# The second block's output product as three fp32r products, with split branches in the merge

## The reference

```python
def first_block(x, c, ...):
    mod = silu(c) @ ada_w + ada_b            # 6 x 1024: shift1, scale1, gate1, shift2, scale2, gate2
    h = rms_norm(x, norm_mix_w) * (1 + scale1) + shift1
    proj = h @ w_in                          # 8-head attention and a gated linear recurrence
    ya, yh = o_att @ w_branch_att, o_hg @ w_branch_hg       # 512 -> 1024 each
    merged = sigmoid(g0) * ya + sigmoid(g1) * yh
    x = x + gate1 * (merged @ w_out)
    h = rms_norm(x, norm_ffn_w) * (1 + scale2) + shift2
    return x + gate2 * expert_choice_ffn(h, ...)   # 16 experts, 64 tokens each, 1024 -> 2048 -> 1024

def second_block(x, ...):
    z = rmsnorm(x, g_mix) @ w_in + b_in
    y = concat(conv_group(z), pool_group(z))       # 512 + 512 features
    h = x + y @ w_out                              # 1024 x 1024, the product of this change
    h = h + swiglu(rmsnorm(h, g_ffn), ...)         # 1024 -> 2816 -> 1024
    return rmsnorm(h, g_final)
```

## Time and profile before

| | us |
|---|---|
| median of 3 runs | 2107.97 (2107.93 to 2111.01) |
| profiled execution | 2108.66 |
| its span, first to last instruction | 2106.9 |
| TensorE busy | 1923.8 (91%) |
| VectorE busy | 670.3 (32%) |
| ScalarE busy | 448.6 (21%) |
| HBM read | 510.00 MB, 243 GB/s over the span |

### The profile page before, as it was taken

How to read it: one execution, slowest core, us unless ns; L and a number is a source line. 1 busy time by engine, 2 the same in 40 slices (tenths; PEclk the granted TensorE clock), 3 DMA queues, 4 the chain that set the end, 5 groups by cost and what they waited for, 6 DMA issues and landing times.

```text
span 2106.9 us, 20424 instructions
## 1 busy us (share of the span) xinstructions
PE 1923.8 (91%) x8738; PEld 1153.0 (55%) x8738; DVE 670.3 (32%) x931; ACT 448.6 (21%) x673; POOL 28.7 (1%) x41
## 2 busy tenths in 40 slices
PE   5999989999689999898988998888899999999998
PEld 5876766567444343343434334342344588888887
DVE  5474474475411110202011010201129623222333
ACT  5357446212211000010100001010020313222222
POOL 0000000000000000000000000000030000000000
PEclk9999999999889999999999999999999999999999
DMA  7311210584669999999999999999951032332311
GB/s 296 97 44 41 63 38 21 202 283 174 259 253 416 417 418 418 417 416 417 416 416 417 418 418 417 417 416 416 380 163 60 20 100 85 96 100 100 100 60 40
DMA packets 149183, 513.42 MB, mean 244 GB/s; under 512 B 8035, under 2 KB 74723, under 8 KB 114147
## 3 DMA queue, kind: packets, MB, share of 16 engines
q1 hardware_dynamic: 144720, 487.95, 59.3%
q10 hardware_dynamic: 4374, 24.18, 3.0%
HBM read 510.00 MB, written 2.10 MB: 243 GB/s over the span
## 4 chain that ended last, share of the span: by engine, by line
PE 67%; DMA 21%; DVE 6%; ACT 4%; issue 2%; SPq 0%; POOL 0%; ACTq 0%; DVEq 0%; POOLq 0%
DMA work<-in_w_exp_up 13%; PE ps L1100 11%; PE ps L1061 6%; DMA ring<-in_w_exp_up 6%; PE ps L1263 5%; PE ps L521 5%; PE ps L1222 4%; PE ps L1223 4%; PE ps L1224 4%; PE ps L537 3%; PE ps L539 3%; PE ps L538 3%; PE ps L988 3%; PE ps L544 3%; PE ps L720 2%
## 5 line engine op out<-in xcount | busy, mean ns | idle before, releaser
L1061 PE MATMUL ps<-work 128*64 128x512 f32 x1208 | 331.4, 595 | 34.9 <-DMA work<-in_w_exp_up 34.9
L1061 PE MATMUL ps<-ring,work 128*64 128x512 f32 x720 | 218.8, 595 | 19.8 <-DMA ring<-in_w_exp_up 19.8
L1061 PEld LDWEIGHTS ps<-work 128*64 128x64 f32 x1208 | 112.0, 137 | 209.5 <-issue 142.3
L2167 DVE TENSOR_TENSOR work<-work,ps 64x512 f32<-64x512 f32 x64 | 42.0, 692 | 495.2 <-ACT work L1629 494.5
L1629 ACT ACTIVATE work<-ps 64x512 f32<-64x512 f32 x64 | 32.6, 584 | 751.1 <-PE ps L1061 751.1
L521 PE MATMUL ps<-work,ring 128*128 128x512 f32 x320 | 138.9, 592 | 0.7 <-issue 0.7
L1100 PE MATMUL ps<-work 128*64 128x512 f32 x568 | 135.4, 630 | 4.2 <-issue 3.6
L1061 PEld LDWEIGHTS ps<-ring,work 128*64 128x64 f32 x720 | 71.7, 137 | 122.8 <-issue 84.4
L1222 PE MATMUL ps<-xh,wh 128*128 128x512 f32 x352 | 137.0, 389 | 0.0
L1224 PE MATMUL ps<-xh,wl 128*128 128x512 f32 x352 | 136.9, 389 | 0.0
L1223 PE MATMUL ps<-xl,wh 128*128 128x512 f32 x352 | 136.9, 389 | 0.0
(11 more groups left out here) (311 smaller groups left out, 2531.7 us busy)
## 6 DMA issues: line engine op xcount, KB each, us to landing
work<-in_w_exp_gate SPq DMA_DIRECT2D x76, 1024.0 KB, 24.5
work<-in_w_exp_up SPq DMA_DIRECT2D x75, 1024.0 KB, 25.9
work<-in_w_exp_down SPq DMA_DIRECT2D x71, 1024.0 KB, 21.0
ring<-in_w_exp_gate SPq DMA_DIRECT2D x45, 1024.0 KB, 24.5
ring<-in_w_exp_up SPq DMA_DIRECT2D x45, 1024.0 KB, 25.5
ring<-in_w_exp_down SPq DMA_DIRECT2D x42, 1024.0 KB, 22.0
ring<-in_w_in SPq DMA_DIRECT2D x27, 1024.0 KB, 6.4
work<-in_ada_w ACTq DMA_DIRECT2D x16, 1024.0 KB, 6.1
```

Of the source, the lines that this page charges most:

```text
L1061: i = e.matmul(PS[64 * gu:64 * gu + 64, fb, :], at(XET + 128 * k + 64 * z, 64), flat(key)[:, 512 * fb:512 * fb + 512], start=(k == 0), sto ...
```

## The change

The second output product takes the split form. Its weights come as four pieces of 512 rows by 512 columns, are cut by ScalarE and VectorE into `O2H` and `O2L`, and y is written twice by ScalarE, raw and high, with the low half from VectorE over the raw tile. The product runs by halves of columns and then tiles of tokens, in the order of tiles `Y_ORDER`; the last pool product moves into its first unit. The branch products of the merge take the same form: `cb_hi`, `cb_lo` split the weights, `OHH`/`OHL` and `OAH`/`OAL` hold the halves of the inputs. The ada row and column products of d = 6 move behind the first two units of the first output product. Half of x is loaded later. The slots' order changes for the experts and the tail. The last expert's down weights go by halves of columns, in rows of 2 KB.

Slots, order of the tail, and SyncE:

```diff
-    cycle = (12, 13, 14, 15, 8, 16, 2, 4, 7, 11, 9, 10, 1, 5, 3, 0, 6)
+    cycle = (2, 13, 12, 16, 15, 8, 7, 11, 14, 4, 9, 10, 1, 5, 3, 0, 6)
...
-    tail = [("i2", c) for c in (3, 1, 2, 0, 5, 4)] + [("o2", n) for n in range(4)] + [("ff", f) for f in range(33)]
-    slots += [0, 1, 2, 3, 4, 5, 0, 1, 2, 3] + [(4, 0, 1, 2, 3)[f % 5] for f in range(33)]
+    tail = [("i2", 3), ("i2", 1), ("o2", 0), ("o2", 1)] + [("i2", c) for c in (2, 0, 5, 4)] + [("o2", 2), ("o2", 3)] + [("ff", f) for f in range(33)]
+    slots += [0, 1, 13, 15, 2, 3, 4, 5, 0, 1] + [4, 5, 4, 5] + [f % 5 for f in range(29)]
...
                 if key == ("wo", 0):
-                    e.wait_ge(s["mg_m"], 1)
+                    e.wait_ge(s["mg_pb"], 6)
...
-                    r0, c0 = 512 * (key[2] % 4), 256 * (key[2] // 4)
-                    for dh in range(2):
-                        src = t["w_exp_down"][NE - 1, r0:r0 + 512, 512 * dh + c0:512 * dh + c0 + 256].rearrange("(k p) n -> p k n", p=128)
-                        e.dma_start(piece(key)[:, 4 * dh:4 * dh + 4, :], src).then_inc(ring[slot], 16)
+                    r0, c0 = 512 * (key[2] % 4), 512 * (key[2] // 4)
+                    src = t["w_exp_down"][NE - 1, r0:r0 + 512, c0:c0 + 512].rearrange("(k p) n -> p k n", p=128)
+                    e.dma_start(piece(key, 4), src).then_inc(ring[slot], 16)
```

TensorE:

```diff
+            def branch(bk, half, j, off, hi, lo, each=None):
+                wl = FWL[plan["cb", half][0]]
+                for k in range(4):
+                    if each is not None:
+                        each(k)
+                    w, x = slice(256 * (off + k) + 128 * j, 256 * (off + k) + 128 * j + 128), slice(512 * k, 512 * k + 512)
+                    e.matmul(bank(bk), CBH[half][:, w], hi[:, x], start=(k == 0), stop=False)
+                    e.matmul(bank(bk), CBH[half][:, w], lo[:, x], start=False, stop=False)
+                    p = e.matmul(bank(bk), wl[:, w], hi[:, x], start=False, stop=(k == 3))
+                return p
...
                     dense_w(b0 + 1, k1, j).then_inc(s["mg_gb"], 1)
-                kb = ("cb", half)
...
                 if j == 0:
-                    e.wait_ge(*got[kb])
-                if d == 6:
...
+                    e.wait_ge(s["fs_l"], (2, 4, 5, 6)[half])
...
+                    e.wait_ge(s["sx_l"], 2)
+                    branch(b0 + 3, half, j, 4, OHH, OHL).then_inc(s["mg_pb"], 1)
+                    branch(b0 + 2, half, j, 0, OAH, OAL, lambda k: e.wait_ge(s["sx_l"], 3 + k)).then_inc(s["mg_pa"], 1)
+                    continue
...
+                branch(b0 + 2, half, j, 0, OAH, OAL).then_inc(s["mg_pa"], 1)
+                if d >= 2:
                     e.wait_ge(s["mg_b"], d - 1)
...
+                branch(b0 + 3, half, j, 4, OHH, OHL).then_inc(s["mg_pb"], 1)
...
+            def second_gate(u):
+                if u == 0:
+                    e.wait_ge(s["d_ada"], 16)
+                    e.wait_ge(s["mg_a"], 8)
+                    ada_row(ACC1, 0, 6)
+                    e.wait_ge(s["mg_b"], 8)
+                    ada_row(ACC1, 512, 7)
+                elif u == 1:
                     e.wait_ge(s["ar_a"], 1)
                     ada_cols(ACC1, 1, 6, 0).then_inc(s["ac_pe"], 1)
...
-            for h in range(2):
-                for n in range(4):
...
+            for a in range(2):
+                for tc in range(TC):
+                    u = 4 * a + tc
+                    o2_free(u)
+                    for n, k in enumerate(Y_ORDER):
+                        q = 2 * a + k // 4
+                        if tc == 0 and n in (0, 2):
+                            e.wait_ge(s["fs_l"], FS_O2 + 2 * a + 2)
+                        if u == 0:
+                            if n == 4:
+                                pool_out(15, 0)
+                            e.wait_ge(s["sx_l"], SXL_O2 + n + 1)
+                        o, w, bk = 128 * tc, slice(512 * (k % 4), 512 * (k % 4) + 512), (0, 1, 2, 3, 6, 7)[u % 6]
+                        e.matmul(bank(bk), YH[:, 512 * k + o:512 * k + o + 128], O2H[q][:, w], start=(n == 0), stop=False)
+                        e.matmul(bank(bk), YH[:, 512 * k + o:512 * k + o + 128], O2L[q][:, w], start=False, stop=False)
+                        p = e.matmul(bank(bk), y_low(k)[:, o:o + 128], O2H[q][:, w], start=False, stop=(n == KD - 1))
                     p.then_inc(s["o2_pe"], 1)
```

ScalarE:

```diff
+            def cb_hi(half, o, n):
+                e.wait_ge(*got["cb", half])
...
+                    e.wait_ge(s["lv_pe"], 52)
+                    e.wait_ge(s["lv_og"], 4)
+                else:
+                    e.wait_ge(s["mg_m"], 4 if half == 2 else 2)
+                e.activation(CBH[half][:, o:o + n], flat(("cb", half))[:, o:o + n], ACT.Copy).then_inc(s["fs_h"], 1)
...
+            def branch_hi():
+                for o in (0, 1024):
+                    cb_hi(0, o, 1024)
+                    yield
+                for o in (0, 1024):
+                    e.activation(OHH[:, o:o + 1024], at(OHG + o, 1024), ACT.Copy).then_inc(s["sx_h"], 1)
+                    yield
...
-            e.dma_start(at(X, 4096).rearrange("p (c d) -> p c d", c=4), xv).then_inc(s["l_x"], 16)
+            e.dma_start(at(X + 2048, 2048).rearrange("p (c d) -> p c d", c=2), xv[:, 2:4, :]).then_inc(s["l_x"], 16)
+            for o in (0, 1024):
+                cb_hi(1, o, 1024)
...
             for d in range(4, 8):
                 i = d - 4
-                if d == 7:
-                    wo_hi(0)
...
                 elif d >= 6:
                     e.wait_ge(s["mg_m"], d - 1)
                 e.activation(at(mt[4 * (d % 2)], 512), bank(4 * (d % 2)), ACT.Tanh, scale=0.5).then_inc(s["mg_sa"], 1)
+                if d in (4, 6):
+                    cb_hi(d // 2, 0, 2048)
+                elif d == 7:
+                    wo_hi(0)
...
+            def o2_hi(i):
+                e.wait_ge(*got["o2", i])
+                if i < 2:
+                    e.wait_ge(s["x_ym"], 34)
+                else:
+                    e.wait_ge(s["i2_pe"], 8)
+                e.activation(O2H[i], flat(("o2", i)), ACT.Copy).then_inc(s["fs_h"], 1)
+            o2_hi(0)
+            o2_hi(1)
...
+                e.activation(YH[:, 2048 + 512 * g:2560 + 512 * g], bank(u % 4), ACT.Copy, scale=vcol("spool", g)).then_inc(s["sx_h"], 1)
                 e.activation(at(YP + 512 * g, 512), bank(u % 4), ACT.Copy, scale=vcol("spool", g)).then_inc(s["po_y"], 1)
...
             for i in range(4):
                 e.wait_ge(s["y_d"], i + 1)
+                e.activation(YH[:, 512 * i:512 * i + 512], at(CV + 512 * i, 512), ACT.Silu, bias=vcol("lnb", i), scale=vcol("lng", i)).then_inc(s["sx_h"], 1)
                 e.activation(at(YC + 512 * i, 512), at(CV + 512 * i, 512), ACT.Silu, bias=vcol("lnb", i),
                              scale=vcol("lng", i)).then_inc(s["y_a"], 1)
-            pool_in(13, 0, 12)
+                if i == 1:
+                    pool_in(13, 0, 12)
             pool_out(14, 1)
             pool_out(15, 0)
```

VectorE:

```diff
+            def cb_lo(half, o, n, count):
+                e.wait_ge(s["fs_h"], count)
+                e.tensor_tensor(FWL[plan["cb", half][0]][:, o:o + n], flat(("cb", half))[:, o:o + n], CBH[half][:, o:o + n].bitcast(F32),
+                                ALU.subtract).then_inc(s["fs_l"], 1)
...
+            for pair in range(4):
+                x = slice(512 * pair, 512 * pair + 512)
+                e.wait_ge(s["at_o"], pair + 1)
+                e.tensor_tensor(OAL[:, x], at(OATT + 512 * pair, 512), OAH[:, x].bitcast(F32), ALU.subtract).then_inc(s["sx_l"], 1)
+            for i in range(2):
+                cb_lo(1, 1024 * i, 1024, i + 3)
...
                     two_ada(d)
+                    if d in (4, 6):
+                        cb_lo(d // 2, 0, 2048, d // 2 + 3)
...
+            def y_lo(*ns):
+                for n in ns:
+                    k = Y_ORDER[n]
+                    e.wait_ge(*((s["y_a"], k + 1) if k < 4 else (s["po_y"], 8 - k)))
+                    e.wait_ge(s["sx_h"], SXH_O2 + n + 1)
+                    e.tensor_tensor(y_low(k), y_raw(k), YH[:, 512 * k:512 * k + 512].bitcast(F32), ALU.subtract).then_inc(s["sx_l"], 1)
+            o2_lo(0)
+            o2_lo(1)
...
+            y_lo(0, 1)
...
+            y_lo(2, 3)
             pool_window(0)
+            y_lo(4, 5, 6, 7)
```

More of the change, by code:

```diff
@@ L119, in ring_plan @@
         n += key[0] != "ada"
-    i = more.index(("c0", 3))
+    i = len(more)
     keys += more[:i] + [("wo", 0)] + more[i:] + [("wo", i) for i in range(1, 4)]
-    slots.insert(len(slots) - len(more) + i, 16)
+    slots.insert(len(slots) - len(more) + i, 14)
     slots += [4, 5, 0]
@@ L1600, in _ @@
             wo_hi(1)
-            for k in range(2, 8):
+            for k in range(2, 7):
                 merged_hi(k)
+            e.wait_ge(s["mg_pa"], 8)
+            e.dma_start(at(X, 2048).rearrange("p (c d) -> p c d", c=2), xv[:, 0:2, :]).then_inc(s["l_x"], 16)
+            merged_hi(7)
             wo_hi(2)
```

(25 more changed lines are left out.)

169 lines of the change are left out of this document (81 added, 88 removed).

## The result

| | before | after |
|---|---|---|
| median, us (7 runs each) | 2108.66 | 2115.28 |
| span of the profiled execution, us | 2106.9 | 2113.8 |
| mean granted TensorE clock | 0.970 | 0.964 |

The ratio is 1.0028, with a 95% interval of 1.0018 to 1.0038: 0.3% slower, 6.6 us. The forecast was 2110.5 us, with a range of 2101.5 to 2118 and 0.33 for slower by over 0.2%; its likeliest case was no measurable change. So the sign of its sum was right, its size 4 us short.

The account below looks back on a forecast made before the run. Bounds by stage: mostly TensorE, the ada loads and VectorE steps early in the merge, weights in the experts. +13.8 - 5.7 + 5 + 1.5 + 3.5 = +18.1, then -15.5: taken as +2.5, 2110.5 us, range 2101.5 to 2118.

Parts of the forecast that it names:

- Merge, d=4: Branch product of d=4 starts at 449.8 us, behind ada step 17 and its weight's split: +13.8 us, attention tail counted in.
- d=0 to 3 gain nothing: Merge: the shorter branch products of d=0 to 3 only lengthen TensorE's wait for the low half at 428.7: 0.
- Merge, d=6: Wait before the d=6 branch products for the split behind ada step 21, its load beside `wo` 0: +5 us.
- Output product: First output product: moved ada row and column products cost 0; first unit waits for the fifth tile's low half, +1.5 us.
- Experts one for one: Experts stay at 60.2 us each, paced by weights; a later start ends the kernel later by the same time.
- Second output product: Second block's output product: 43.5 us in place of 55.51, earlier start, shorter work behind it; -15.5 us in all.
- Last down weights: Last expert's down product is TensorE's own work and waits for no weights: value 0, bounds 0 and -0.4 us.
- Clock: Slow matmuls behind the two new TensorE waits cost 2.1 and 1.4 us: +3.5 us.
- The splits arrive in time: Rival: the merge's low halves are ready as TensorE comes, so nothing is lost: 2088 us, chance 0.06.
- The ada chain shortens: Rival: step 17 comes at 442 and the d=6 wait shrinks to 2 us: 2102.5 us, chance 0.14.
- The product gains less: Rival: ScalarE's doubled writes and VectorE's low halves hold the second output product's first unit 4 us more: 2114.5 us, chance 0.08.
- The waits cost more: Rival: d=6 wait of 7.5 to 8 us, clock low about 7 us after both waits: 2116.3 us, chance 0.22.

Follow-up runs that it names:

- e4: The changed kernel with branch weight 2's split moved: high half before the load of ada 16, low half between ada steps 14 and 15; 2098.1 us, ratio 0.9939.
- e7: e4 with the 32 one-column ada products parted, 16 behind the second unit of the first output product and 16 behind the third; 2100.3 us, ratio 0.9953.
- e2: The kernel before with only the new merge and what goes with it, without the new second output product and last down weights; 2129.5 us, ratio 1.0090.
- e1: The kernel before with only the second output product changed; 2094.7 us, ratio 0.9924.
- e12: e9 with the d=6 second gate piece's low halves ahead of the d=5 merge, and both halves of y at multiples of 64 bytes; 2087.3 us, ratio 0.9896.
- e3: The kernel before with only the last expert's down weights going by halves of columns in rows of 2 KB; 2111.1 us, ratio 1.0004.
- e8: e4 with the two low halves for the gate products of d=4 made between ada steps 12 and 13 on VectorE; 2100.0 us, ratio 0.9960.
- e10: e1 with the two low halves for the gates of d=4 made between ada steps 12 and 13 on VectorE; 2094.6 us, ratio 0.9924.
- e5: e4 with the low half of branch weight 3 ahead of ada steps 20 and 21 on VectorE; 2095.7 us, ratio 0.9937.
- e6: e5 with the loads of ada 20 and 21 issued behind the high half of branch weight 3 on ScalarE; 2094.9 us, ratio 0.9932.
- e9: The changed kernel with the edits of e5 to e7 and the other merge splits moved ahead of ada steps; 2091.3 us, ratio 0.9910.

## Why the prediction was right or wrong

**Merge, d=4: right.** 449.8 us forecast, 450.22 measured, after ada step 17 at 445.49 (445.1 forecast) and a low half of 2.29 us. e4 shows that the queue was the cause. The first ada load of the chain starts at 395.15 instead of 393.74, 1.4 us later where +1.0 stood for the attention's tail, and takes 11.40 us instead of 13.95; which part of the change made it shorter was not tested.

**d=0 to 3 gain nothing: right**, by the wait that grew from 2.47 to 7.18 us.

**Merge, d=6: size within its bounds, cause half wrong.** The wait is 3.62 us, within the +3 to +7.5 given around +5. The step said that ada 21 would hold the low half, because `wo` 0 would make its load take 10 to 12 us. The chain of the changed kernel says otherwise:

```profile
474.95 9.72 DMA ring<-in_w_branch_hg
484.69 1.92 ACT cbh L1559
486.70 2.31 DVE fwl L2087
489.05 0.79 PE ps L877
```

Step 21 started 8.3 us after its load was issued (474.31) and was over at 484.95. What came last was the branch weight's own load, 9.72 us beside 3 MB of ada and output weights, and then both halves in series. An estimate from these rows: behind step 21 alone the low half would have ended at 487.2, and TensorE came at 485.43, so 1.8 of the 3.62 us are the step's and the rest is the load's. That step 21 starts 32.4 us after the d=4 product, within the forecast 31.2 to 33.2, is luck: its load went out 24.1 us after that product, not 21.2, and was faster than forecast.

**Output product: the term that failed.** The ada row and column products "only move behind the output product's first units: 0". They do move, and the sum up to the first unit is right: 13.8 - 5.7 + 5 + 3.5 less the 3.4 us of products that leave d=6 is 13.2, and the unit starts at 512.57 instead of about 499.6, 13 us later. (The closeness is in part luck: the wait of d=6 was 1.4 us shorter than its term and the d=4 start 0.5 us later than its own.) The wait in the first unit is 1.39 us, near the +1.5. But at their new place both groups of 16 one-column products stand together, and 2.2 us of slow matmuls follow; before, each group of 16 stood alone (480.06 and 511.06 us) and nothing slow followed. e7 shows the difference in the rows. The groups together take 4.1 us where two took 1.7 us each, 0.7 us more. With 0.8 us in the routing (the last unit's addition is 20.8 us late, the gather 21.6) that makes 3.7 us, against the 3.5 us between +18.1 and +21.6 before the experts. The products of this step were put at 0 without a row for their new place; they cost 2.9 us.

**Experts one for one: right.** 21.6 us at the first gather, 21.4 at the last down product, 60.2 us per expert. e2 shows that nothing of it comes back.

**Second output product: mechanism right, one term mis-sized.** -15.5 forecast, -14.1 measured in the whole change, -14.0 in e1. A unit takes 5.60 us, not 5.44: 8 by 0.16 = 1.3 us. The wait in the first unit is 0.2 us instead of 0.6. From the last product to the transposes it takes 3.24 us (1738.65 to 1741.89), where 3.25 was forecast. On the product alone the rows forecast 12.0 us; eight units of 5.60 us save 10.7, and eight of 5.44 us (e12) would save the 12.0. The estimate by the four passes of the Trainium skill, page "FP8 and Floating Point Precision", section "TensorE Precision Notes", was 13.9 us of 55.51; no run reached it. What the overhead is that the prediction gives as the reason is not shown: the rows give 0.227 us for an fp32r matmul and 0.859 us for a plain one, no more.

**Last down weights: right**, 0 (e3), though they land at 395 instead of 341 GB/s.

**Clock.** After the two waits of 12.27 and 3.62 us there are 9 and 6 steps of 0.43 us, at a granted clock of 0.50, 1.8 and 1.2 us lost, near the 2.1 and 1.4 of the sum. What it lacked was the third place, behind the one-column products.

**The rivals.** "The splits arrive in time" gave 2088 us, and it is what the reordered kernels reach (2091.3 and 2087.3): its mechanism was right for another order of the same instructions, which the prediction didn't weigh. "The ada chain shortens" did not come: step 17 is at 445.49, not 442. "The product gains less" did not either, for its reason: the first unit waits 0.2 us, and what is missing is the 1.3 us of the addresses. "The waits cost more" named the d=6 split as the place and 2116.3 us; the time is near it, the place is not.

## What to carry to other kernels

A product in a cheaper form needs its operands split first, and the split runs on in-order engines: before counting the gain, find what stands ahead of each split in VectorE's and ScalarE's lists, and put it ahead of those that wait for a load. Where TensorE waits at several places for one in-order chain, moving one split alone may only move the wait (e8, e10); e4 paid because the wait that it removed, 12.27 us, was far longer than what came back behind it (0.88 us). The edits after e4 are worth 1 to 4 us each, near what the medians of these runs can tell, so they were judged by the waits in the traces. Tiny products should not end up side by side: here the slow steps behind them cost 1.0 to 2.4 us.

## What the runs showed of the hardware

- A three-matmul product costs 5.60 us for 24 matmuls of 512 columns with 20 stationary operands 32 bytes off a multiple of 64, 5.49 to 5.50 with 4, and 5.44 with none. The first 16 cost 6 to 7 ns each, the last 4 more, about 13 ns, so the cost isn't simply so much for each. e12 moved other things too, but its step of the unit is read from the product itself. Only these two offsets were tried. The address is not the only thing that does this: in the merge the branch products of d=5 take 0.227 us a matmul in the attention's half (468.83 to 471.55) and 0.233 in the recurrence's (471.55 to 474.35), and all their operands lie at multiples of 64 bytes; why is open.
- 32 one-column products in a row (3.5 to 4.1 us) are followed by steps of 0.43 us, the spacing of 1.2 GHz, in all six kernels that have the row: 11 of them in the changed kernel, 12 in e8, 7 in e2, 5 in e4, e5 and e6. Behind 16 of them (1.7 us) there is none, in before, e7, e9 and e12.
- The order of issue between two queues changes when a load lands, even at under 1 us. The same 0.5 MB piece, issued by SyncE 0.1 to 0.7 us after ScalarE had issued two ada loads of 1 MB each, landed 9.7 to 10.2 us after its issue (the changed kernel, e2, e4, e7, e8). Issued 0.7 us ahead of them it landed within 7.9 us (e5), and within 5.6 us where they went out over 5 us later (e9, e12).
